# Two decoder layers with a 32-expert stage: earlier expert weights, a seventh place for them, a routing table in two passes, and head norms spread by bf16 parts

## What is computed

```python
# head norms: mean over a head's columns, for each token and head
hm = rmsnorm(hm, mlstm_norm_w)            # 4 heads of 128 ("mn")
qd = partial_rope(rmsnorm(qd, q_norm_w))  # 8 half-heads of 64 ("qk", with kd)
kd = partial_rope(rmsnorm(kd, k_norm_w))
hd = rmsnorm(diff_attention(qd, kd, vd), subln_w)      # 4 heads of 128 ("dn")
merged = sigmoid(g_m) * (hm @ w_br_m) + sigmoid(g_d) * (hd @ w_br_d)
x = x + gate1 * (merged @ w_out)
h2 = rmsnorm(x, norm2_w) * (1 + scale2) + shift2
# router: best of 4 groups, in it the best 2 of 8 experts; 32 experts
for e in range(32):
    y = y + combine[:, e:e+1] * ((silu(h2 @ w_gate[e]) * (h2 @ w_up[e])) @ w_down[e])
x = x + gate2 * y
```

## Time and profile before

| | us |
|---|---|
| median of 3 runs | 1700.73 (1693.45 to 1703.79) |
| the profiled execution | 1698.56 |
| its span, first to last instruction | 1696.6 |
| PE, DVE, ACT busy | 1581.3, 819.4, 541.5 |

### The profile page before, as it was taken

The page is one execution under the profiler, slowest core; times in us unless marked ns, Lnnn a source line. Parts: engine busy times, 40 slices in busy tenths (PEclk is TensorE's granted clock), DMA queues, the critical chain, the costliest instruction groups (busy, mean ns, idle before and its releaser), DMA issues.

```text
span 1696.6 us, 19976 instructions
## 1 busy us (share of the span) xinstructions
PE 1581.3 (93%) x8159; PEld 1194.8 (70%) x8159; DVE 819.4 (48%) x1414; ACT 541.5 (32%) x878; POOL 83.4 (5%) x107
## 2 busy tenths in 40 slices
PE   7999999999999999999998999999999994888865
PEld 7987777777787788888886787797678872333322
DVE  6556334355365766775223963436662734222121
ACT  5334444444434322222113523322353331111110
POOL 5000000000000000000000010000000001121111
PEclk9999999999999999999999999999999996989998
DMA  5335221212333466554222232211114527999995
GB/s 163 113 100 134 67 61 64 75 53 72 75 100 113 136 223 223 192 190 139 99 100 72 75 100 87 87 51 62 64 50 149 218 110 305 399 412 403 403 409 192
DMA packets 147089, 260.45 MB, mean 154 GB/s; under 512 B 16585, under 2 KB 121333, under 8 KB 133681
## 3 DMA queue, kind: packets, MB, share of 16 engines
q1 hardware_dynamic: 138544, 241.41, 40.4%
q0 software_dynamic: 8448, 17.70, 3.6%
HBM read 253.79 MB, written 15.25 MB: 159 GB/s over the span
## 4 chain that ended last, share of the span: by engine, by line
PE 82%; DVE 8%; issue 4%; ACT 2%; DMA 2%; POOL 0%; POOLq 0%; DVEq 0%; ACTq 0%
PE psum L2390 20%; PE psum L2391 19%; PE psum L2392 19%; PE psum L2954 6%; PE psum L2971 4%; PE psum L2696 1%; PE psum L2685 1%; PE psum L2668 1%; PE psum L2932 1%; DMA Xg<-h_rows,tok 1%; DVE cst L1938 1%; DVE WL L1511 1%; PE psum L2595 1%; ACT Sb L1070 1%; DVE qkm L1725 1%
## 5 line engine op out<-in xcount | busy, mean ns | idle before, releaser
L2390 PE MATMUL psum<-AHs,WH 128*128 128x512 f32 x744 | 306.0, 411 | 7.7 <-DVE WL L1511 5.2
L1511 DVE TENSOR_TENSOR WL<-raw,WH 128x2048 fp32r<-128x2048 f32 (+1 forms) x100 | 226.7, 2267 | 178.2 <-ACT WH L985 177.8
L2391 PE MATMUL psum<-ALs,WH 128*128 128x512 f32 x744 | 292.8, 393 | 0.0
L2392 PE MATMUL psum<-AHs,WL 128*128 128x512 f32 x744 | 292.7, 393 | 0.0
L985 ACT ACTIVATE WH<-raw 128x2048 fp32r<-128x2048 f32 (+1 forms) x100 | 189.0, 1890 | 139.1 <-PE psum L2392 106.1
L2390 PEld LDWEIGHTS psum<-AHs,WH 128*128 128x128 f32 x744 | 141.3, 190 | 43.5 <-DVE WL L1511 6.1
L2390 PE MATMUL psum<-AH,WH 128*128 128x512 f32 (+1 forms) x464 | 169.2, 365 | 0.0
L2391 PE MATMUL psum<-AL,WH 128*128 128x512 f32 (+1 forms) x464 | 164.0, 353 | 0.0
L2391 PEld LDWEIGHTS psum<-ALs,WH 128*128 128x128 f32 x744 | 141.6, 190 | 30.9 <-issue 3.1
L2392 PE MATMUL psum<-AH,WL 128*128 128x512 f32 (+1 forms) x464 | 163.1, 352 | 0.0
L2392 PEld LDWEIGHTS psum<-AHs,WL 128*128 128x128 f32 x744 | 141.3, 190 | 30.8
(11 more groups left out here) (540 smaller groups left out, 2292.8 us busy)
## 6 DMA issues: line engine op xcount, KB each, us to landing
raw<-w_in SPq DMA_DIRECT2D x45, 1024.0 KB, 5.2
WE<-w_gate SPq DMA_DIRECT2D x34, 1024.0 KB, 21.1
WE<-w_up SPq DMA_DIRECT2D x34, 1024.0 KB, 24.1
WE<-w_down SPq DMA_DIRECT2D x34, 1024.0 KB, 22.7
araw<-w_ada SPq DMA_DIRECT2D x24, 1024.0 KB, 5.6
raw<-w_ffn_in SPq DMA_DIRECT2D x22, 1024.0 KB, 7.9
raw<-w_ffn_out SPq DMA_DIRECT2D x11, 1024.0 KB, 4.8
raw<-w_out SPq DMA_DIRECT2D x8, 1024.0 KB, 5.1
```

Source lines behind the costliest of these rows:

```text
L1511: V.tensor_tensor(WL[:, n, 0:w], raw[:, n, 0:w], WH[:, fed[0] % HL, 0:w].bitcast(F32), ALU.subtract).then_inc(S_("lo_ready"), 1)
L2390: MM(dst, lh, rh, start=first, stop=False)
L2391: MM(dst, lh, rl, start=False, stop=False)
L2392: return MM(dst, ll, rh, start=False, stop=last)
```

## The change

1. **Earlier pieces.** SP loads three of the six pieces of pair 2 during the last two slabs of `w_out`, a fourth at the end of the dense work, and only two behind `h2_stored`.
2. **Seven gate and up places.** Gate and up weights go round seven places in the order of halves; down weights keep six. The seventh, `WE6`, lies over `xtm`, so pair 3's loads wait until `out` is set (`out_set`).
3. **Two passes.** A first pass makes the table for all pairs but the overflow's, from rank and home alone. The second (overflow) runs behind it; `overflow_ready`, for which SP waits with pair 3, now comes after the first turned rows are copied. POOL gathers 0 and 1 first and sets `out` behind them. The weights of the tokens are worked out during pair 0.
4. **Bf16 parts.** The reciprocals are cut into three bf16 parts that add up to the float32 value. PE turns them (4 small bf16 matmuls each), ACT copies the rows to SBUF, and one bf16 matmul of 512 columns by a 0/1 selector adds the parts and spreads a row. `MN_SPREAD` and `DN_SPREAD` go one piece later.

```diff
-SLOTS = 6
+SLOTS, GU_SLOTS = 6, 7
+HOME = 1024.0
-    ids = ... + r[None, None, :] + 1
+    ids = ... + r[None, None, :] - int(NOBODY)
-MN_SUMS, QK_SUMS, MN_SPREAD, ROPE_AT, DIFF_AT, DN_SUMS, DN_SPREAD = 27, 26, 32, 34, 43, 63, 65
+MN_SUMS, QK_SUMS, MN_SPREAD, ROPE_AT, DIFF_AT, DN_SUMS, DN_SPREAD = 27, 26, 33, 34, 43, 63, 66
+        GU = [w[:, 0:KC * 2 * DE] for w in WE] + [at("WE6", 111.8125, [KC * 2 * DE])]
+        TILES = [(t, half) for t in range(NPAIR) for half in range(2 if t < BASE else 1)]
+        def gate_up_slot(t, half):
+            return TILES.index((t, half)) % GU_SLOTS
         def load_gate_up(sp, t, half, e):
-            n = (2 * t + half) % SLOTS
-            if t >= SLOTS // 2:
-                sp.wait_ge(*when("gu_done", t - SLOTS // 2 + 1))
+            x = TILES.index((t, half))
+            if x >= GU_SLOTS:
+                sp.wait_ge(*when("gu_done", TILES[x - GU_SLOTS][0] + 1))
+            for g in range(2):
+                load_gate(sp, t, half, e, g)
+            slab_consumed(sp, SLAB_OF[("wo2", 1)])
+            load_gate(sp, 2, 0, 2, 1)
+            slab_consumed(sp, SLAB_OF[("wo2", 2)])
+            load_down(sp, 2, 0, 2)
+            load_gate(sp, 2, 1, NE // 2 + 2, 0)
             sp.wait_ge(*when("dense_ready", len(GROUPS)))
             load_expert(sp, 1, 1, 1)
+            load_gate(sp, 2, 0, 2, 0)
             sp.wait_ge(*when("h2_stored", 16 * NB))
-            load_expert(sp, 2, 0, 2)
+            load_gate(sp, 2, 1, NE // 2 + 2, 1)
             sp.wait_ge(*when("n_two_summed", 1))
-            load_expert(sp, 2, 1, NE // 2 + 2)
+            load_down(sp, 2, 1, NE // 2 + 2)
             sp.wait_ge(*when("overflow_ready", 1))
-            load_pair(sp, OVER, [sp.value_load(...) for x in range(2)])
+            over = [sp.value_load(...) for x in range(2)]
+            sp.wait_ge(*when("out_set", 16 * NB))
+            load_pair(sp, OVER, over)
...
 # POOL
-            for t in range(NB):
-                pool.dma_start(out[0, P * t:P * t + P, :], xtm[:, t, :]).then_inc(S_("out_set"), 16)
             pool.wait_ge(*when("h2_stored", 16 * NB))
             pool.wait_ge(*when("tokens_ready", 1))
             gather(0)
             gather(1)
+            for t in range(NB):
+                pool.dma_start(out[0, P * t:P * t + P, :], xtm[:, t, :]).then_inc(S_("out_set"), 16)
+            pool.wait_ge(*when("over_tokens", 1))
...
 # ACT
+            def rows_copied(tag, b, n, dst):
+                act.wait_ge(*when(tag + "_turned", 1))
+                nc.scalar.activation(dst[0:n, :], bank(b)[0:n, :], ACT.Copy).then_inc(S_(tag + "_rows"), 1)
...
 # DVE, last flow
+            def in_parts(tag, x, dst, rest):
+                dve.wait_ge(*when(tag + "_rms", 1))
+                link(V.tensor_copy(dst[:, :, 0], x))
+                link(V.tensor_tensor(rest, x, dst[:, :, 0], ALU.subtract))
+                link(V.tensor_copy(dst[:, :, 1], rest))
+                link(V.tensor_tensor(rest, rest, dst[:, :, 1], ALU.subtract))
+                V.tensor_copy(dst[:, :, 2], rest).then_inc(S_(tag + "_parts"), 1)
-                if at_ == MN_SPREAD - 1:
+                if at_ == MN_SPREAD - 2:
                     inverse("mn", small[:, 120:136])
                     inverse("qk", small[:, 136:200])
+                    in_parts("mn", ...)
+                    in_parts("qk", ...)
...
 # PE, last flow
+            def turned_parts(tag, b, src, n):
+                pe.wait_ge(*when(tag + "_parts", 1))
+                for t in range(NB):
+                    ins = MM(bank(b, P, P * t)[0:n], src[:, t].rearrange("p n c -> p (n c)"), identb, start=True, stop=True)
+                ins.then_inc(S_(tag + "_turned"), 1)
             def head_spread(tag, b):
-                pe.wait_ge(*when(tag + "_rms", 1))
+                pe.wait_ge(*when(tag + "_rows", 1))
                 for c in range(C1):
-                    for t in range(NB):
-                        ins = MM(bank(b + c, P, P * t), rms16[:, NB * c + t:NB * c + t + 1].to_broadcast([P, P]), ident,
-                                 start=True, stop=True)
+                    ins = MM(bank(b + c), sel1[0:3 * C1, c:c + 1].to_broadcast([3 * C1, P]), rowst[0:3 * C1, :], start=True, stop=True)
             def qk_spread(c):
-                for t in range(NB):
-                    for j in range(2):
-                        ins = MM(bank(2 + c % 2, P, P * t)[DH * j:DH * j + DH], r1, ident, start=True, stop=True)
+                MM(bank(2 + c % 2), sel2[0:48, c, :], rowst2[0:48, :], start=True, stop=True).then_inc(S_("qk_bc"), 1)
+                if at_ == MN_SPREAD - 1:
+                    turned_parts("mn", 2, parts1, 3 * C1)
+                    turned_parts("qk", 3, parts2, 48)
                 if at_ == MN_SPREAD:
                     head_spread("mn", 4)
...
 # PE, expert stage (DVE's pairs() is changed in the same way)
             def pairs(t0, t1):
                 transpose_rows(t0)
+                if t0 == 0:
+                    overflow_spots()
                 for t in range(t0, t1):
                     gate_up(t)
                     if t + 1 < t1:
                         transpose_rows(t + 1)
+                    if t == 0:
+                        weights_by_row()
                     transpose_act(t)
                     down(t)
```

More of the change, by code:

```diff
@@ L916, in _, with rows_of_pair @@
                                    ).then_inc(S_(f"max_landed{h % 2}"), 16)
+            def rows_of_pair(t):
+                return (tok if t < BASE and t != OVER else tok2)[:, t:t + 1]
             def gather(t):
@@ L937, in scatter @@
                         pool.wait_ge(*when(f"y_stored{t % 2}", y_stores(t) - 16))
-                    rows = tokover[:, half:half + 1] if t == OVER else tok[:, t:t + 1]
+                    rows = tokover[:, half:half + 1] if t == OVER else rows_of_pair(t)
                     pool.indirect_dma_start(out=out[0], out_offset=bass.IndirectOffsetOnAxis(ap=rows, axis=0),
@@ L2250, in _, with chosen, full_blocks @@
[L2250 to L2252 removed]
+            at_pair = [P, 2 * NB, NPAIR]
+            def chosen(dst, x, tmp):
+                link(V.tensor_tensor(tmp, ohs, x.to_broadcast(wide), ALU.mult))
+                link(V.tensor_reduce(dst, tmp, AX_X, ALU.add))
+            def full_blocks(dst, x, limits, tmp):
+                n = x.shape[1]
+                link(V.tensor_tensor(tmp[:, 0:n, :], x.unsqueeze(2).to_broadcast([P, n, 7]),
+                                     limits.unsqueeze(1).to_broadcast([P, n, 7]), ALU.is_ge))
+                link(V.tensor_reduce(dst, tmp[:, 0:n, :], AX_X, ALU.add))
@@ new lines, in token_of @@
+            def token_of(dst, b):
+                found = bank(b, 2 * NPAIR).rearrange("p (c n) -> p c n", c=2)
+                link(V.tensor_scalar(spot, found[:, 0, :], NOBODY, None, ALU.add))
+                return V.tensor_tensor(dst, spot, found[:, 1, :], ALU.add)
+            by_tile = [r8[:, n] for n in range(9)]
+            rkh, rk, home, pair, bs, blk, ov_, more, w1_ = [x.rearrange("p c t -> p (c t)") for x in by_tile]
+            chosen(by_tile[3], places[:, 1, :].unsqueeze(1).unsqueeze(1), prod[0])
```

262 lines of the change are left out of this document (151 added, 111 removed).

## The result

The changed kernel takes 1683.53 us (median of 6 runs, 1679.93 to 1684.45), the kernel before in the same sessions 1700.51 (1693.45 to 1703.79): ratio 0.9902, 95% interval 0.9887 to 0.9918, or 17.0 us less. The profiled execution took 1684.45 us, its span 1682.7: 14.1 us and 13.9 us under those of before. The forecast was 1679, the range 1671 to 1689.

What follows compares the result with a forecast made beforehand. The prediction took PE to bound the kernel up to 1390 us and the saturated stream of weights to set the end. From 1698.56 us, -7.8 (spreads) and -11.9 (stream) gave 1678.9, stated as 1679, range 1671 to 1689.

Steps and rivals of the forecast that it cites:

- The spreads, -7.8: Last flow: spreading mn, dn and qk by bf16 matmuls saves PE 9.9 us, less 2.1 us of new waits.
- wait (a): Piece 31: DVE has ten more small operations, so PE waits 0.6 us at piece 32's start, bounds 0 and 1.5.
- wait (b): Piece 35: PE waits 1.5 us at `qk_swap` until DVE has finished `qk_normed`.
- The old wait: Last flow: PE's existing wait of 1.28 us for the roped rows stays, as DVE and PE move together.
- The clock falls in piece 35: Rival, last flow: 9 us of dense work at half speed costs 4.5 us, total 1683 us; chance 0.17.
- The gather starts 6.4 us earlier: Routing: the shorter DVE chain lets the first gather start at 1408.0 us instead of 1414.42.
- The landing, 6.2: First gather: 6.2 us to landing, the middle of 8.6 and 3.8; landed at 1414.2, 8.8 us earlier.
- The estimate by turns: First gather: if DMA engines alternate queues packet by packet, it takes 5.1 us and the total is 1.1 us less.
- First down at 1434.7: Expert stage: pair 0's first down is done at 1434.7 us instead of 1442.94.
- The stream, -11.9: Expert stage: the stream of weights starts 1.7 us earlier and is 10.2 us shorter.
- The seventh place does nothing: Rival: `out_set` or overflow numbers come after 1434, pair 3's first half loads no earlier; 5.1 us, total 1684; chance 0.08.
- The clock falls at every pair: Rival, expert stage: waits for weights lower PE's clock, 3.8 us a fall; 12 falls give 1712 us; chance 0.03.

Runs made afterwards that it cites:

- the spreads alone: Part 4 (bf16 parts, ACT copies, selectors, later spreads) alone on the kernel before; ratio 0.9953 (0.9937 to 0.9969).
- `out` first: Changed kernel with pair 2's last two pieces issued behind the overflow numbers, so first gathers and the setting of `out` have the DMA engines; ratio 0.9892.

## Why the prediction was right or wrong

The time lies in the range, 4.5 us above the forecast, and at the border between "faster by over 1%" and "within 1%" (0.9902, the interval on both sides of 0.99). Both halves came out smaller than forecast, the stream by a third, so the nearness owes something to the medians, which show 3 us more than the profiled pair. The bound was right: the stream is last, and PE's savings in the stage count next to nothing (6 us on the first down gave 1.3 at the last pair). Step by step:

- **The spreads, -7.8.** Right: the flow is 7.6 us shorter wherever the clock stays up. The terms: mn 1.7 (1.8 forecast), dn 2.2 (2.1; with the spreads alone 0.32 and 0.96 where there were 3.48), a chunk of qk 0.71, so 5.7 (6.0), wait (a) none (0.6), wait (b) 1.38 (1.5). They add up to 8.2; the 0.6 to the measured 7.6 is not placed. The old wait stayed (1.3 us at the roped rows).
- **The clock falls in piece 35.** It did not in any profile with the new spreads; the wait of 1.38 us left it up. But a fall came elsewhere: behind the 32 one-column sums of "dn", in six of eight profiles with the new spreads and the sums in one run, in none of two with the old spreads, and in none of three with "dn" spread out. It costs 236.5 - 235.0 = 1.5 us. Why the same 32 matmuls lower the clock in some runs only is open, and with so few profiles their part in it is likely and not proved. So the profiled flow is 6.0 shorter: of the missing 1.8, 1.5 is a clock fall that I had sought only where PE waits, not where it works on single columns.
- **The gather starts 6.4 us earlier.** It started 19.4 us behind the end of the dense work instead of 24.7: 5.4. The first pass is as long as forecast plus 1.0 us for which DVE waits on the ranks. `h2_stored` came 18.5 us behind the dense work, 1.4 later than before, within the worst bound.
- **The landing, 6.2.** This step failed, as a size: 8.89. I took the middle between two ends, when the row nearest to the case was the loaded one: 2 MiB ahead cost as much (8.1 to 8.9 in five profiles) as the six of before. The estimate by turns from the Trainium skill ("DMA: Bandwidth & Descriptors", Queues, rings and completion order), 5.1 us, took equal bytes per turn; the page says packets. The trace disagrees with the estimate: 8.9 us. The gather's 0.5 MiB in it was too much as well, by the rows some 0.3 MB.
- **First down at 1434.7**, 45.0 behind the dense work: it was 48.6. Of the 3.6 us, 1.0 is the start and 2.7 the landing.
- **The stream, -11.9.** 7.8. Counted as I did, from the first down, it starts 1.9 us later than before instead of 1.7 earlier, and from there it is 9.6 us shorter (10.2). But the experiments show that this was the wrong place to count from. With the first down 6 us earlier the last pair gained 1.3. What holds in the six profiles without a hole is 235.3 to 235.5 us from pair 3's issue, and what the queue loses behind it is added. "From 1434.7 it has always something to issue" is true; what was missed are the 3.6 us lost around that, some 2 of them in holes, since SP can't queue ahead of a place, and that `out_set` (35 us, where I had put it at 30) would be the next to be late. With `out` first the last pair is at 270.3, the forecast's 1659.8 - 1389.7 = 270.1, but that came another way: the first down there ends 42.6 us behind the dense work, not 45.0.
- **The seventh place does nothing.** It does: 2.9 us of stage, less than the 5.1 put on it. Pair 3 is issued 6.5 us earlier, and 3.5 of them are lost behind the issue.
- **The clock falls at every pair.** No: of four waits for weights one was followed by a fall (in the other profiles one to three of five or six, in that of before none of six). The rule of the Trainium skill ("TensorE: Matmul & The Clock Gate", HAM oscillation), written for short bursts and taken over to the pairs by the prediction, would have every one start slow; the trace does not agree, and only a fall in the last pair (8.7 to 8.8 us, in three of the runs) reached the end.

## What to carry to other kernels

When a saturated stream sets the end, take one distance from the trace (first issue without a hole to last use) and add to it every interval in which the queue is empty: moving a consumer earlier is worth little until the loads can be issued earlier (6 us gave 1.3 here). An order of loads is judged by what stands ahead of the one small transfer that all wait for; with 2 MiB ahead, a gather of some 0.3 MB took 8.1 to 8.9 us instead of 3.6 to 3.8. If a place comes free only when a store has landed, give that store the engines first and let the loads that have a place already fill its gap: 3.9 us of the stage in one trace, too little for the medians to confirm.
